# Half-length Fourier tables with mirrored outputs in a diffusion block on 8 cores

## The reference

```python
def fourier_mix(u):
    bsz, t, _ = u.shape
    ug = u.astype(jnp.float32).reshape(bsz, t, FOURIER_GROUPS, FOURIER_GROUP_DIM)
    y = jnp.fft.fft2(ug, axes=(1, 3), norm="ortho").real
    return y.reshape(bsz, t, FOURIER_WIDTH).astype(u.dtype)
```

## Time and profile before

| what | value |
|---|---|
| time, median of 3 runs | 1517.73 us (1517.01 to 1519.97) |
| the profiled execution's own time | 1518.2 us |
| its span on core 7, the slowest | 1516.5 us |
| PE busy on core 7 | 1123.9 us, 74% of the span |
| ACT, DVE, POOL busy | 652.4, 533.5, 143.2 us |
| share of PE in the chain that ended last | 65% |
| mean granted TensorE clock, core 7 | 0.885 of full speed |

### The profile page before, as it was taken

One profiled execution on the slowest core, in us unless ns is written; L12 is line 12 of the kernel. 1 busy time (PEld: TensorE's weight loads), 2 busy tenths in 40 slices (PEclk: granted clock), 3 DMA queues, 4 the chain that ended last, 5 costly groups with the idle time before them and its releaser, 6 DMA issues.

```text
span 1516.5 us, 18964 instructions; the slowest of 8 cores (1501.6 to 1516.5 us)
## 1 busy us (share of the span) xinstructions
PE 1123.9 (74%) x5360; PEld 506.0 (33%) x5360; DVE 533.5 (35%) x711; ACT 652.4 (43%) x894; POOL 143.2 (9%) x136
## 2 busy tenths in 40 slices
PE   0112499986666676664899998749999986999993
PEld 0111144432222222222344443314434432444441
DVE  1011130024767766774422323323330214331204
ACT  2554120009887588973132216644441323442221
POOL 0451000000000000000121121000000221000203
PEclk9955799998787887877999999969999997999997
DMA  8994603322221202214521305444475426467432
GB/s 220 323 311 130 215 1 111 111 70 90 91 85 61 62 31 90 91 56 153 160 98 49 111 1 180 180 143 151 152 244 194 146 84 222 152 187 245 140 112 111
DMA packets 53831, 203.35 MB, mean 134 GB/s; under 512 B 6104, under 2 KB 6488, under 8 KB 52704
## 3 DMA queue, kind: packets, MB, share of 16 engines
q1 hardware_dynamic: 46816, 176.97, 37.0%
q0 software_dynamic: 6912, 25.17, 4.2%
HBM read 176.94 MB, written 25.17 MB: 133 GB/s over the span
## 4 chain that ended last, share of the span: by engine, by line
PE 65%; ACT 12%; DMA 10%; issue 5%; DVE 4%; POOL 2%; SPq 1%; DVEq 0%; ACTq 0%; POOLq 0%
PE bank L253 65%; DMA pt<-pos 4%; ACT thr L266 3%; DMA stg<-win 2%; ACT mult L266 2%; ACT aa L266 1%; ACT xs L266 1%; DMA stg<-wmod 1%; DVE x1y L277 1%; DMA stg<-wout 1%; POOL x1y L274 1%; ACT L266 1%; POOL xt L274 1%; SPq L249 1%; ACT hT L266 1%
## 5 line engine op out<-in xcount | busy, mean ns | idle before, releaser
L253 PE MATMUL bank<-hT,w1t 128*128 128x512 bf16 x1024 | 225.1, 383 | 31.9 <-DVE w1t L294 17.7
L253 PE MATMUL bank<-w2t,hid 128*128 128x512 bf16 x1024 | 224.7, 383 | 6.7 <-ACT w2t L266 6.7
L253 PEld LDWEIGHTS bank<-hT,w1t 128*128 128x128 bf16 x1024 | 100.9, 99 | 155.9 <-issue 37.8
L253 PEld LDWEIGHTS bank<-w2t,hid 128*128 128x128 bf16 x1024 | 100.9, 99 | 130.5 <-issue 12.2
L253 PE MATMUL bank<-hT,wug 128*128 128x512 bf16 x512 | 118.2, 385 | 19.4 <-DMA stg<-wlru 19.4
L266 ACT ACTIVATE rl<-bank 128x512 bf16<-128x512 f32 x128 | 76.5, 598 | 130.2 <-PE bank L253 117.2
L253 PE MATMUL bank<-xc,wgt 128*128 128x512 bf16 (+1 forms) x160 | 50.6, 398 | 108.6 <-ACT thr L266 102.0
L274 DVE TENSOR_TENSOR hid<-rl 128x512 bf16<-128x512 bf16 x128 | 54.2, 424 | 130.4 <-ACT rl L266 130.3
L253 PE MATMUL bank<-ctab,Z 128*128 128x512 bf16 x256 | 97.0, 379 | 0.0
L253 PE MATMUL bank<-stab,Z 128*128 128x512 bf16 x256 | 97.0, 379 | 0.0
L266 ACT ACTIVATE w2t<-stg 128x1024 bf16<-128x1024 f32 x32 | 33.6, 1056 | 136.4 <-DVE w2t L294 125.6
(11 more groups left out here) (110 smaller groups left out, 1399.8 us busy)
## 6 DMA issues: line engine op xcount, KB each, us to landing
stg<-w SPq DMA_DIRECT2D x128, 512.0 KB, 4.4
stg<-wmod SPq DMA_DIRECT2D x48, 512.0 KB, 5.9
stg<-win SPq DMA_DIRECT2D x36, 512.0 KB, 4.9
xt<-x SPq DMA_DIRECT2D x16, 512.0 KB, 18.2
pt<-pos SPq DMA_DIRECT2D x16, 512.0 KB, 17.1
xp_scr<-xt POOLq DMA_DIRECT2D x16, 512.0 KB, 9.1
ctab<-ctab SPq DMA_DIRECT2D x4, 2048.0 KB, 11.3
stab<-stab SPq DMA_DIRECT2D x4, 2048.0 KB, 17.6
```

What stands on the lines that cost most here:

```text
L253: return P.op(PE, lambda e: e.matmul(out, lhsT=lhsT, rhs=rhs, start=start, stop=stop), reads, writes)
```

## The change

The tables keep their first two blocks of output positions, 0 to 1023. For each of these two blocks and each group, P and Q are accumulated in two banks instead of one. ACT copies P into a new float32 tile `psb`; DVE writes `psb + Q` to the positions of the block, and `psb - Q`, with a step of -1, to the mirrored positions. Position 1024 has no partner; it is made apart, ahead of the block loop, by 64 matmuls with a moving operand of 2 columns, `cnq`, whose first column is the alternating sign. One more small load brings `cnq`, ahead of the first load of `wf`. Blocks 2 and 3 of the tables are neither made nor loaded.

```diff
+    cnq = A.alloc("cnq", [128, 2], BF16)
+    R_cnq = Res("cnq")
+    dma(SP, cnq[:], cn_d, writes=[R_cnq], sem="const")
+    psb = [A.alloc("psb", [128, 512], F32) for _ in range(2)]
+    R_psb = [Res("psb%d" % i) for i in range(2)]
     load_w(wf[0][:], win_d[16], 8, 128, R_wf[0], [DVE])
...
-    for kt in range(4):
-        s = kt % 2
-        if kt >= 2:
-            dma(SP, ctab[s][:], ct_d[kt], writes=[R_ctab[s]])
-            dma(SP, stab[s][:], st_d[kt], writes=[R_stab[s]])
+    pnq, R_pnq = nbank()
+    for g in range(4):
+        for j in range(16):
+            mm(pnq[:, 2 * g:2 * g + 2], Z[:, j, g, 0:128], cnq[:], j == 0, j == 15, [R_Z[g], R_cnq], [R_pnq])
+    act(yfT[:, :, 1024:1025], pnq[:, 0:8:2].rearrange("p (g o) -> p g o", o=1), AF.Identity, [R_pnq], R_yf)
+    YTOT = 4 * T
+    for kt in range(2):
         for g in range(4):
-            pb, R_pb = nbank()
+            pP, R_pP = nbank()
             for j in range(16):
-                mm(pb[:], Z[:, j, g, 0:128], ctab[s][:, j, :], j == 0, False, [R_Z[g], R_ctab[s]], [R_pb])
-                mm(pb[:], Z[:, j, g, 128:256], stab[s][:, j, :], False, j == 15, [R_Z[g], R_stab[s]], [R_pb])
-            if g % 2 == 0:
-                act(yfT[:, g, kt * 512:(kt + 1) * 512], pb[:], AF.Identity, [R_pb], [R_yf[g]])
+                mm(pP[:], Z[:, j, g, 0:128], ctab[kt][:, j, :], j == 0, j == 15, [R_Z[g], R_ctab[kt]], [R_pP])
+            pQ, R_pQ = nbank()
+            for j in range(16):
+                mm(pQ[:], Z[:, j, g, 128:256], stab[kt][:, j, :], j == 0, j == 15, [R_Z[g], R_stab[kt]], [R_pQ])
+            u = (kt * 4 + g) % 2
+            act(psb[u][:], pP[:], AF.Identity, [R_pP], [R_psb[u]])
+            tt(DVE, yfT[:, g, kt * 512:(kt + 1) * 512], pQ[:], psb[u][:], ALU.add, [R_pQ, R_psb[u]], [R_yf[g]])
+            if kt == 0:
+                outm = bass.AP(yfT, g * T + (T - 1), [[YTOT, 128], [-1, 511]])
+                tt(DVE, outm, psb[u][:, 1:512], pQ[:, 1:512], ALU.subtract, [R_pQ, R_psb[u]], [R_yf[g]])
             else:
-                copy(DVE, yfT[:, g, kt * 512:(kt + 1) * 512], pb[:], [R_pb], [R_yf[g]])
+                outm = bass.AP(yfT, g * T + 1536, [[YTOT, 128], [-1, 512]])
+                tt(DVE, outm, psb[u][:], pQ[:], ALU.subtract, [R_pQ, R_psb[u]], [R_yf[g]])
```

More of the change, by code:

```diff
@@ L213, in build_program @@
     fc_d = din("fc", [128, 256], BF16)
-    ct_d = din("ctab", [4, 128, 16, 512], BF16)
-    st_d = din("stab", [4, 128, 16, 512], BF16)
+    ct_d = din("ctab", [2, 128, 16, 512], BF16)
+    st_d = din("stab", [2, 128, 16, 512], BF16)
+    cn_d = din("cnyq", [128, 2], BF16)
     ident_d = din("ident", [128, 128], BF16)
@@ L952, in lay @@
     def lay(m):
-        return np.ascontiguousarray(m.reshape(16, 128, 4, 512).transpose(2, 1, 0, 3)).astype(bf)
-    return fc.astype(np.float32).astype(bf), lay(ctab), lay(stab)
+        return np.ascontiguousarray(m.reshape(16, 128, 4, 512).transpose(2, 1, 0, 3)[0:2]).astype(bf)
+    cn = np.zeros((128, 2), np.float32)
+    cn[:, 0] = ((-1.0) ** np.arange(128)) / math.sqrt(T)
+    return fc.astype(np.float32).astype(bf), lay(ctab), lay(stab), cn.astype(bf)
 def _kp(w, nblk, bw):
@@ L978 @@
     if "consts" not in _CACHE:
-        fc, ctab, stab = _dft_tables()
-        _CACHE["consts"] = dict(pos=_pos_table(), fc=fc, ctab=ctab, stab=stab,
+        fc, ctab, stab, cnyq = _dft_tables()
+        _CACHE["consts"] = dict(pos=_pos_table(), fc=fc, ctab=ctab, stab=stab, cnyq=cnyq,
                                 ident=np.eye(128, dtype=np.float32).astype(ml_dtypes.bfloat16),
```

## The result

The changed kernel takes 1473.09 us (median of 9 runs) against 1517.87 us (median of 10) for the kernel before. The ratio is 0.9703, 95% interval 0.9693 to 0.9714: 45 us less, where 47 were forecast. The profiled execution took 1474.05 us with a span of 1472.5 us on core 3, which is the slowest core here; before it was core 7. Executions in which one die or both ran over 1% longer at a lower granted clock are left out, and of the second profile of the kernel before, where cores 0 to 3 show a granted clock of 0.81 for 470 to 538 us, only cores 4 to 7 are used.

A forecast was written before the change was run, and what follows sets the result against it. PE's gapless matmul stream in the Fourier stage was taken as the bound. Removed matmuls (-55.25 us) plus load, block with wait, clock and evictions summed to -47.09 us, giving 1471.0 us, range 1466 to 1476.

The forecast's parts named there:

- What bounds the kernel: Fourier stage: PE's gapless matmul stream sets the time; 256 of 512 table matmuls go at 0.2158 us each, 55.25 us less.
- The added load: Ahead of the weights and tables: one more load issue moves everything behind it by 0.38 us, bounds 0 and 0.78.
- The 64 small matmuls: Ahead of the table loop: 64 two-column matmuls at 0.0266 us each, 1.70 us of work.
- Rival C: Small-matmul block: weight loads don't overlap, so it costs 6.4 us instead of 5.24; 1472.3 us in all, chance 0.08.
- The wait: Inside the small-matmul block: PE waits 3.54 us for DVE's last copy into Z's group 3; 5.24 us with the work.
- Rival A: Small-matmul block costs its instructions alone, no wait and no fall of the clock: 1465.9 us, chance 0.07.
- The clock: Behind the wait: granted clock falls to 0.50 for a stretch, costing the table matmuls 1.68 us, bounds 0 and 3.4.
- The evictions: Add and mirrored subtract, 0.69 us each on DVE: seven pairs hidden behind PE, the last adds 0.86 us before the barrier.
- The sum: Whole kernel: -55.25 + 0.38 + 5.24 + 1.68 + 0.86 = -47.09 us.
- the one that gave later stages nothing: Stages behind C: banks shift by one, each still waiting for a bank freed 7 turns before; priced at nothing.
- rival B: Stage C or those behind: clock comes back late, three half-rate stretches cost 5.0 us; 1474.4 us, chance 0.12.

The follow-up runs named there:

- half kernel: Kernel before with only the first two of its four table blocks, positions 1024 to 2047 zeroed, nothing added: 1461.65 us, ratio 0.9649.
- fill: Changed kernel plus 16 unused full table matmuls between the third and fourth group of small matmuls: 1468.04 us, ratio 0.9689 to the kernel before.
- block-alone kernel: Kernel before plus the cnq load and the 64 small matmuls ahead of its loop, all four table blocks kept: 1525.12 us, ratio 1.0066.
- mid_x4: Changed kernel with the 64 small matmuls moved between the two table blocks and made four times: 1472.16 us, ratio 0.9710 to the kernel before.
- nyq_mid: Changed kernel with the 64 small matmuls moved from ahead of both table blocks to between them: 1465.48 us, ratio 0.9669 to the kernel before.
- sub12: Changed kernel with each mirrored subtract made twelve times over: 1502.58 us, ratio 0.9912 to the kernel before.

## Why the prediction was right, point by point

1. **What bounds the kernel.** Right. Everything taken from PE's stream in stage C left the stage: 55.3 us for 256 matmuls in the half kernel against 55.25 forecast. Two readings of the rows were loose, and nothing rests on them: the ninth slice has PE at 8 tenths, and core 1's clock of 0.99 comes from the end of its window, which lies behind its last table matmul at 316; its stream too ran at 1.00.
2. **The added load.** 0.47 us of issue against 0.38; that it reaches the end was not shown.
3. **The 64 small matmuls.** 1.70 forecast, 1.7 as the difference of two stage C lengths, 1.60 in the trace of the moved block. Rival C is out: the lengths of the weight loads don't add up.
4. **The wait.** Loop start minus block start is 219.35 - 214.23 = 5.12 us against 5.24. From the 48th small matmul's start to the 49th's it takes 3.54 us, so the wait is 3.51 counted as the forecast counts its 3.54, from where the 49th would have started; the 3.38 is what PE's records leave idle. The wake-up was 0.14 us here instead of the 0.24 taken. Rival A is out, and moving the block shows the wait's removal.
5. **The clock.** 1.68 forecast. In the changed kernel the loop takes from 219.35 to 276.37 on core 3, 57.02 us where 255 x 0.2158 + 0.38 = 55.41 would do: 1.61. Six of the eight cores have one stretch of 3.4 us. Two have 6.8, which begins inside the wait, and lose 2.9 us in the loop; the bound was 3.4. `fill` shows that the idle time is what it follows here. That small matmuls can do the same was not in the prediction; at 64 of them, behind a stream at full rate, it played no part.
6. **The evictions.** Both operations 0.69 us, no price for the step, seven pairs hidden. The gap between them was 0.10 us, not the 0.17 of the earlier trace rows, so the last pair adds 0.79 instead of 0.86.
7. **The sum.** Forecast -47.09; by ratio 45 us. The terms inside stage C are right to 0.1 us together, and each of them nearly so by itself. Stage B's first matmul on core 7 starts at 282.0, where 282.6 was forecast. The step that was too small is the one that gave later stages nothing: B to E are longer by 1.0, 0.8 and 1.2 us in the changed kernel, as means over the cores. Of the 1.2 in stage E, 0.8 is the last output transfer, which lands later in every kernel here that loads two table blocks, and not in the block-alone kernel; the other 0.4 goes with 0.6 us more at a granted clock of 0.50. Of the 0.8 in stage D, 0.5 is the wait for the first weights of the MLP (14.2 us from the last matmul before it to the first behind it, 14.7 in the changed kernel). The 1.0 in stage B has no such account. Within one kernel a longer B can go with more time at 0.50 (367.9 us with 146 of it and 373.0 with 158 in the kernel before), but between kernels it doesn't: with the wait filled B has 157 us of it as a mean and lasts 370.2, in the kernel before 153 and 369.8. Shifted banks are excluded. The place in DRAM is excluded for the last transfer alone. What makes these stages longer in every variant stays open; rival B named the mechanism of the clock, but its 5 us were too much (its sum is -43.7, not -43.8). As times, the missing 2 us lie within what a kernel differs by from itself (0.24%), so it is the traces alone that show them.

## What to carry to other kernels

A stage between two barriers that one engine fills without a gap can be costed from start-to-start times, to 0.1 us in 48 here. Before new work is put ahead of a loop, look at what the loop's first iterations have been hiding: the block of 1.7 us cost 6.7, because it asked for the last group's data at once and idle time lowered the clock behind it; one table block later it costs 1.7. A kernel run against itself gave 0.24% here, so a residue of that size is to be sought in the stages of the traces, on all cores, and not in the times.

## What the runs showed of the hardware

- Matmuls with 2 moving columns and full 128-column weights run 0.0250 us from start to start at a granted clock of 1.00 and 0.0267 at 0.50 (`mid_x4`, all cores but core 5, which has a gap of 0.12 us in the second part; 0.0266 at 1.00 in the earlier trace rows), though each weight load is recorded with 95 to 108 ns.
- A gapless run of 6.5 us of such matmuls lowered the granted clock to 0.50 on all 8 cores; 1.6 us of them did not on any.
- In `nyq_mid` two cores of a die had a third level of granted clock, 0.81, in stage B: from 279.6 to 441.5, with stretches at 0.50 between. In `sub12` cores 2 and 3 had it from 569 to 731. Eight cores at once had run the table stream at 1.00, so a dense stream on all of them did not by itself bring it; what does was not tested. The windows of core 0:

```profile
292.70:309.60 16.90, 7.37 (x17) 1.98 (x17) 10.69 (x7) 16.63 (x19) 0.00 (x0) 0.50 0.56 172
309.80:340.00 30.20, 25.96 (x130) 11.41 (x130) 16.70 (x17) 21.74 (x26) 0.00 (x0) 0.81 0.00 1
```

These two cores have the longest stage B of that run, 378.9 and 376.5 us, against 372.3 as the mean of the other six; that is why this kernel has the longest B in the table.
